# Weight passes that run from the last column to the first, in a four-layer trunk on one core

## The reference, cut to what matters

```
for i in range(4):
    x = x + 0.5 * swiglu(rms_norm(x, norm_ffn1[i]), w_gate, w_up, w_down)
    x = x + mixer_i(rms_norm(x, norm_mix[i]))          # fox, conv, diff, fox
    x = x + 0.5 * swiglu(rms_norm(x, norm_ffn2[i]), w_gate, w_up, w_down)

swiglu(h, w_gate, w_up, w_down) = (silu(h @ w_gate) * (h @ w_up)) @ w_down
```

## Time and profile before

| what | value |
|---|---|
| median of three runs | 1987.56 us (1984.85 to 1987.9) |
| profiled execution: span from the first to the last instruction | 1984.6 us |
| TensorE busy | 1955.5 us, 99% of the span |
| TensorE weight loads, beside the matmuls | 1717.6 us, 87% |
| VectorE busy | 1420.7 us, 72% |
| ScalarE busy | 1044.4 us, 53% |
| moved by DMA | 350.14 MB, a mean of 176 GB/s |

### The profile page before, as it was taken

How to read it: one execution, slowest core, us unless ns; L and a number is a source line. 1 busy time by engine, 2 the same in 40 slices (tenths; PEclk the granted TensorE clock), 3 DMA queues, 4 the chain that set the end, 5 groups by cost and what they waited for, 6 DMA issues and landing times.

```text
span 1984.6 us, 29082 instructions
## 1 busy us (share of the span) xinstructions
PE 1955.5 (99%) x12574; PEld 1717.6 (87%) x12574; DVE 1420.7 (72%) x1645; ACT 1044.4 (53%) x1250; POOL 101.6 (5%) x114
## 2 busy tenths in 40 slices
PE   7999999999999998999999999999999999999999
PEld 6888889888888896988888888788888888888887
DVE  7776678875787565877587658887758765778763
ACT  6554566554555344654465455575436544566542
POOL 3000001000200001100100000010000000001000
PEclk9999999999999998999999999999999999999999
DMA  7655434655665683665656553356566655435653
GB/s 238 194 183 182 149 128 154 192 188 189 192 191 180 201 249 83 191 191 182 200 191 192 177 184 128 107 176 191 183 196 190 191 183 180 148 128 171 191 189 107
DMA packets 336365, 350.14 MB, mean 176 GB/s; under 512 B 10077, under 2 KB 331886, under 8 KB 336238
## 3 DMA queue, kind: packets, MB, share of 16 engines
q1 hardware_dynamic: 331742, 343.58, 54.1%
q10 hardware_dynamic: 4496, 4.70, 1.2%
HBM read 346.04 MB, written 2.22 MB: 175 GB/s over the span
## 4 chain that ended last, share of the span: by engine, by line
PE 94%; DVE 3%; ACT 2%; issue 1%; POOL 1%; DMA 0%; ACTq 0%; DVEq 0%; POOLq 0%
PE banks L1443 49%; PE banks L1448 24%; PE banks L1434 5%; PE banks L1436 5%; PE banks L1435 5%; PE banks L1901 1%; PE banks L1660 1%; PE banks L1713 1%; ACT sb_w_high L470 1%; DVE sb_w_low L808 1%; PE banks L1680 1%; PE banks L1697 1%; ACT sb_scores L598 0%; PE banks L1818 0%; PE banks L1667 0%
## 5 line engine op out<-in xcount | busy, mean ns | idle before, releaser
L808 DVE TENSOR_TENSOR sb_w_low<-sb_raw,sb_w_high 128x2048 fp32r<-128x2048 f32 (+1 forms) x332 | 749.5, 2262 | 208.8 <-ACT sb_w_high L470 208.2
L1443 PE MATMUL banks<-sb_x_both,sb_w_high 128*128 128x512 f32 x2816 | 721.9, 393 | 1.9 <-ACT sb_w_high L470 1.9
L470 ACT ACTIVATE sb_w_high<-sb_raw 128x2048 fp32r<-128x2048 f32 (+1 forms) x332 | 618.5, 1867 | 122.2 <-DMA sb_raw<-in_ffn_w_down 109.0
L1443 PEld LDWEIGHTS banks<-sb_x_both,sb_w_high 128*128 128x128 f32 x2816 | 500.2, 189 | 82.2 <-ACT sb_w_high L470 2.3
L1448 PEld LDWEIGHTS banks<-sb_x_both,sb_w_low 128*128 128x128 f32 x2792 | 386.5, 188 | 35.2
L1448 PE MATMUL banks<-sb_x_both,sb_w_low 128*128 128x256 f32 x2792 | 394.6, 279 | 0.0
L1443 PE MATMUL banks<-sb_h_both,sb_w_high 128*128 128x512 f32 x1408 | 360.2, 395 | 0.0
L1443 PEld LDWEIGHTS banks<-sb_h_both,sb_w_high 128*128 128x128 f32 x1408 | 250.8, 188 | 45.3
L1448 PEld LDWEIGHTS banks<-sb_h_both,sb_w_low 128*128 128x128 f32 x1408 | 190.9, 188 | 16.9
L1448 PE MATMUL banks<-sb_h_both,sb_w_low 128*128 128x256 f32 x1408 | 194.4, 279 | 0.0
L488 ACT ACTIVATE sb_x_both<-sb_xT,sb_vec 128x256 fp32r<-128x256 f32 x96 | 43.3, 501 | 200.8 <-DVE sb_xT L841 176.1
(11 more groups left out here) (229 smaller groups left out, 1936.6 us busy)
## 6 DMA issues: line engine op xcount, KB each, us to landing
sb_raw<-in_ffn_w_gate SPq DMA_DIRECT2D x88, 1024.0 KB, 5.4
sb_raw<-in_ffn_w_up SPq DMA_DIRECT2D x88, 1024.0 KB, 5.3
sb_raw<-in_ffn_w_down SPq DMA_DIRECT2D x64, 1024.0 KB, 5.0
sb_raw<-in_ffn_w_down SPq DMA_DIRECT2D x32, 768.0 KB, 4.3
sb_raw<-in_fox_w_in SPq DMA_DIRECT2D x24, 1024.0 KB, 5.2
sb_raw<-in_conv_w_pw SPq DMA_DIRECT2D x12, 1024.0 KB, 5.4
sb_raw<-in_diff_w_in SPq DMA_DIRECT2D x12, 1024.0 KB, 5.0
sb_raw<-in_fox_w_out SPq DMA_DIRECT2D x8, 1024.0 KB, 4.8
```

The source lines that it names most:

```text
L470: act.activation(slot(w_high, b)[:, 0:width(b)], slot(raw, b)[:, 0:width(b)], ACT.Copy).then_inc(S["high_ready"], 1)
L808: dve.tensor_tensor(slot(w_low, b)[:, 0:width(b)], slot(raw, b)[:, 0:width(b)], slot(w_high, b)[:, 0:width(b)].bitcast(F32), ALU.subtract) ...
L1443: return pe.matmul(pair(bank[at][:, :]), high[:, n * P:(n + 1) * P], m_both, start=first, stop=last, skip_group_check=True)
```

## The change

In the helpers of the weight passes, the free axis of the moving operand and of the destination is reversed. Column 255 of the moving operand is read first and its sum is written first, to the place where it stood before; column 0 comes last. In `on_both`, the high part still comes ahead of the low part, and each of the two runs of 256 is reversed in itself. The stationary operands, the semaphores, and the number and order of the instructions stay as they are. Line 1579 and all matmuls outside the helpers stay as they are too.

```diff
             def three_passes(dst, s_high, s_low, m_high, m_low, first, last, loose=False):
+                dst, m_high, m_low = dst[:, ::-1], m_high[:, ::-1], m_low[:, ::-1]
                 pe.matmul(dst, s_high, m_high, start=first, stop=False, skip_group_check=loose)
                 pe.matmul(dst, s_high, m_low, start=False, stop=False, skip_group_check=loose)
                 return pe.matmul(dst, s_low, m_high, start=False, stop=last, skip_group_check=loose)
...
             def on_both(at, n, high, m_both, first, last):
 
-                return pe.matmul(pair(bank[at][:, :]), high[:, n * P:(n + 1) * P], m_both,
+                return pe.matmul(pair(bank[at][:, :])[:, :, ::-1], high[:, n * P:(n + 1) * P], m_both[:, :, ::-1],
                                  start=first, stop=last, skip_group_check=True)
 
             def on_high(at, n, low, m_high):
 
-                pe.matmul(bank[at][:, SEQ:2 * SEQ], low[:, n * P:(n + 1) * P], m_high,
+                pe.matmul(bank[at][:, SEQ:2 * SEQ][:, ::-1], low[:, n * P:(n + 1) * P], m_high[:, ::-1],
                           start=False, stop=False, skip_group_check=True)
```

## The result

The changed kernel takes 2020.01 us (median of four runs, 2019.72 to 2021.12) against 1987.3 us for the kernel before, a ratio of 1.0168 with a 95% interval of 1.0154 to 1.0183. It is slower by 33 us. The forecast was no change.

A forecast was written before the change was run, and what follows sets the result against it. The prediction took TensorE's matmul pace as the bound and added 0 us to the 1984.6 us span; with 3.0 us around the profiled span it forecast 1987.5 us, no change, with a stated range of 1960 to 3610 us.

The forecast's parts named there:

- The bound: Whole kernel: TensorE, busy 99% of the span, sets the time by its matmuls' number and pace; 1% of pace is 18 us.
- The exposed work: Weight passes at lines 1434 to 1436, 1443 and 1448: 11,304 matmuls, 1800 us, 91% of the span, all on the path.
- I take 0 us: Weight-pass matmuls: reading and writing columns backwards costs nothing, since jumps in the read address cost nothing visible; 0 us.
- jumps in the address: 512-column matmuls read two separated runs, yet pay 229 and 233 ns against 232 for two single runs.
- the argument from neighbouring pairs: PSUM writes: backward columns still come in neighbouring pairs sharing a line, so by the rule's reason nothing changes.
- A change of the access order has no collision to relieve: Weight passes: TensorE does the same number of matmuls with every DMA engine moving and with none.
- either window: The stretches 786 to 788 us (DMA at 0.00) and 790 to 792 us (DMA at 0.99), each with 19 matmuls.
- Half pace: All weight-pass matmuls: reversed ones stream one column at a time, 1539 to 1619 us more, 3527 to 3607 us; chance 0.27.
- The price per matmul: All 11,304 weight-pass matmuls: a reversed run starts dearer by 11.3 ns, 128 us in all, 2115 us; chance 0.14.
- my own range for no change: Kernel time if direction costs nothing: 1983 to 1992 us around 1987.5.

The follow-up runs named there:

- e1: The changed kernel with only the moving operand read backwards and the sums written forwards: 2021.27 us, ratio 1.0168.
- h2: Against the kernel before, weight passes take groups of four columns (16 bytes) from last to first, forwards inside each group: 2021.95 us, ratio 1.0176.
- h3: Against the kernel before, weight passes take groups of four columns from first to last, backwards inside each group: 1987.55 us, ratio 1.0003.
- f6: The kernel before (forward reads) with x_both 64 bytes higher in SBUF, at 0 modulo 256: 2008.28 us.
- h1: The kernel before (forward reads) with everything from the first weight tensor on 64 bytes higher in SBUF: 1987.01 us, ratio 0.9994.
- e2: The changed kernel with only the sums written backwards and the moving operand read forwards: 1985.58 us, ratio 0.9991.
- g1: The changed kernel with the stationary operand of on_high cut from 128 to 32 columns: 2018.22 us, ratio 1.0152.
- g2: The kernel before (forward reads) with the stationary operand of on_high cut from 128 to 32 columns: 1995.52 us, ratio 1.0037.
- h4: Against the kernel before, only the 512-column matmuls of on_both run backwards, read and write: 2003.45 us, ratio 1.0083.

## Why the prediction was wrong, step by step

- *The bound* was right: TensorE's pace is the time, a per cent of it is worth 18 us, and nothing hides it. The 33.6 us of span are 1.9% of the 1800 us of weight passes.
- *The exposed work* was right: the same counts at the new paces give the loss to about 1 us, once the distances left out are taken in. One pace was read a little high: the earlier trace rows have eight steps in 0.95 us, which is 119 ns rather than 118, and over the whole trace the three-pass matmuls stand at 116.3 and 115.6 ns. That moves the 1800 us by 5 and the forecast by nothing.
- *"I take 0 us"* is the step that failed, for the read. I argued it from jumps in the address, which cost nothing visible. A backward read costs 33 us here: 4.8 and 3.8 ns per matmul on x, 0.4 and 2.4 on h (e1). The runs show that what counts is the order in which the 16-byte groups are read (h2, h3) and how the moving operand lies to the rest, most likely to the weights (f6, h1). The trace had a sign that the pace of one instruction isn't fixed: pieces of eight at 0.91 and at 0.94 us in turn, the two tiles of a block. I took their middle, 116 ns, where I should have asked what makes the difference.
- For the write, 0 was right (e2), and the argument from neighbouring pairs fits that, though no run tests it.
- *"A change of the access order has no collision to relieve"* went too far. The earlier trace rows have 19 matmuls in either window, one more or less would be 5%, and the loss is 1.7%: they can't exclude so small an effect of the neighbours' traffic. The means within one tile, above, do: they differ by 0.3 ns at most, and the loss per `on_high` on x is 3.8. Neither says anything about TensorE's two reads, of the moving and of the stationary operand, and these run in every row of the kernel. The Trainium skill's page "TensorE: Matmul & The Clock Gate", section "Step-by-step: what each phase is for", gives these reads two independent ports, so that a weight load takes no read bandwidth from the running matmul. f6 against h1 (2008 and 1987 us, with `x_both` at the same place and only what else moved differing) speaks against full independence.
- *The rivals.* Half pace, with 0.27 the largest, is excluded by every run: no group of the weight passes went at half pace. The time does lie within the stated 1960 to 3610 us, but only because that range was stretched to take in the half pace; my own range for no change ended at 1992. The price per matmul was the right family, for which I had 0.14. Its mean is 33.6 us / 11,304 = 3.0 ns, not 11.3, and it is no price of a run's start: 4.8 ns on one group of 512-column matmuls and 0.4 ns on the other.
- The kernel's text had the hint that the profile lacks: tensors that serve only to shift others. I read past them. Forward reads at three other addresses of `x_both` take 2004 to 2008 us, which is 17 to 21 of the 33 us. So half of the loss or more can be put down to a good place that the tensors give and the change spoils; that is a reading of four addresses and not a measured share.

Open is what meets inside the engine. No run took the weight load away altogether, g1 and g2 did not isolate it, and h4 shows that a matmul's pace depends on its neighbours' direction too. Nor is it only addresses modulo 256. Within a run of eight `on_both` on x in the kernel before, every operand's address steps by a multiple of 256 bytes, and still the distances go in threes: 229, 232 and 227 ns. The weights of a block's two tiles lie 512 bytes apart and their `on_high` go at 117.5 and 114.0 ns; whether that distance, the PSUM bank or what ran before decides was not tried. Whether backward reads would reach 1987 us if `h_both`, `o_high` and the weights were moved as well was not tried; at the six addresses of `x_both` they do not. No version beat the kernel before.

## What to carry to other kernels

Where TensorE is the bound, the place of the moving operand relative to the others is worth 1% here (1987 to 2008 us with forward reads), without any change of work. So any edit that moves a buffer, resizes one ahead of it or changes the order of reading has to be timed for that alone. Read the pace from the chain, and when one instruction shows two paces in turn, take it as a sign that its pace can move, and time a version with the operand at another address. A reversed write, and a reversed order within 16 bytes, cost nothing here.

## What the runs showed of the hardware

- 512-column float32r matmuls ran at 229.0 to 235.0 ns and 256-column ones at 114.6 to 120.0, at a granted 2.4 GHz, with the same work, depending on the operands' addresses, on the direction of the read and, in h4, on that of the neighbours.
- For backward reads the dependence on the moving operand's address repeats after 256 bytes (192, 448 and 704 modulo 1024 give the same paces, to 0.1 ns) and not after 128 (2026.93 us at 0, 2013.08 at 128).
- It goes by the relation to what else lies in SBUF, and not by the address itself: 1987.01 us with all moved by 64 bytes, 2008.28 with `x_both` alone.
- Writing the sums backwards costs nothing (1985.58 us, 0.9991, 0.9982 to 1.0001), nor does a reversed order within 16 bytes (1987.55 us).
- A stationary operand of 32 columns in place of 128 shortened the load's record from 188 to 108 ns and didn't speed up the matmuls that used it (116.7 ns against 115.8).
